# First mixers' attentions: the low part's subtraction issued in the step of the high part's copy

## The reference

```python
def hybrid_mixer(x, w_in, b_in, ...):
    proj = x @ w_in + b_in
    (qa, ka, va, beta_raw, a_raw, za, qb, kb, vb, qc, kc, vc) = jnp.split(proj, split_at, axis=-1)
    o_a = gated_deltanet(qa, ka, va, beta_raw, a_raw, za, conv_w, a_log, dt_bias, gdn_norm_g)
    o_b = chunk_relpos_attention(qb, kb, vb, rel_bias)
    o_c = swa_sink_attention(qc, kc, vc, sinks)
    gates = jax.nn.sigmoid(x @ w_gate + b_gate).reshape(b, t, N_BRANCH, d)
    merged = (gates[:, :, 0] * (o_a @ w_br_a) + gates[:, :, 1] * (o_b @ w_br_b)
              + gates[:, :, 2] * (o_c @ w_br_c))
    return merged @ w_out
```

## Time and profile before

| what | us |
|---|---|
| median of 3 runs | 2250.28 |
| lowest, highest | 2248.72, 2250.85 |
| the profiled execution's own time | 2246.99 |
| span of its instructions | 2245.2 |
| PE busy | 2217.0 (99%) |
| DVE busy | 1632.4 (73%) |
| ACT busy | 1197.9 (53%) |
| attentions of layer 0, first to last subtraction (L1636) | 348.0 to 399.6 |
| attentions of layer 1, the same | some 820 us later |

### The profile page before, as it was taken

One profiled execution on the slowest core, in us unless ns is written; L12 is line 12 of the kernel. 1 busy time (PEld: TensorE's weight loads), 2 busy tenths in 40 slices (PEclk: granted clock), 3 DMA queues, 4 the chain that ended last, 5 costly groups with the idle time before them and its releaser, 6 DMA issues.

```text
span 2245.2 us, 34615 instructions
## 1 busy us (share of the span) xinstructions
PE 2217.0 (99%) x14127; PEld 1903.4 (85%) x14127; DVE 1632.4 (73%) x2508; ACT 1197.9 (53%) x1896; POOL 129.6 (6%) x185
## 2 busy tenths in 40 slices
PE   9999999999999999999999999999999999989999
PEld 7888899878888888888898778888888888867887
DVE  5777768868676776768668867776877678666776
ACT  5555446645555545555356544655554655556653
POOL 2100010120000000000100110000000000420000
PEclk9999999999999999999999999999999999999999
DMA  7755564445556556655554446655655656643654
GB/s 243 226 188 192 188 222 122 146 142 188 190 187 192 187 186 209 192 190 195 196 181 140 140 143 210 196 188 170 215 174 171 213 188 190 200 134 117 197 176 150
DMA packets 284207, 408.17 MB, mean 182 GB/s; under 512 B 13828, under 2 KB 171072, under 8 KB 283792
## 3 DMA queue, kind: packets, MB, share of 16 engines
q1 hardware_dynamic: 276096, 380.84, 52.9%
q0 software_dynamic: 7808, 25.04, 3.8%
q10 hardware_dynamic: 144, 0.07, 0.0%
HBM read 403.98 MB, written 1.91 MB: 181 GB/s over the span
## 4 chain that ended last, share of the span: by engine, by line
PE 91%; DVE 5%; ACT 2%; DMA 1%; issue 1%; POOL 0%; SPq 0%; DVEq 0%; ACTq 0%
PE PS L575 24%; PE PS L506 13%; PE PS L513 12%; PE PS L507 12%; PE PS L574 11%; PE PS L472 3%; PE PS L473 2%; PE PS L474 2%; PE PS L577 2%; PE PS L558 1%; PE PS L556 1%; PE PS L557 1%; PE PS L492 1%; DVE WL L1391 1%; DVE QX L1698 1%; ACT WH L1007 1%
## 5 line engine op out<-in xcount | busy, mean ns | idle before, releaser
L1391 DVE TENSOR_TENSOR WL<-RW,WH 128x1024 fp32r<-128x1024 f32 (+2 forms) x678 | 806.6, 1223 | 160.4 <-ACT WH L1007 156.1
L575 PE MATMUL PS<-XT,WH 128*128 128x512 f32 x2368 | 808.0, 394 | 0.0
L1007 ACT ACTIVATE WH<-RW 128x1024 fp32r<-128x1024 f32 (+2 forms) x678 | 680.5, 1042 | 200.2 <-DMA RW<-in_w_in 40.2
L574 PE MATMUL PS<-XT,WL 128*128 128x256 f32 x2072 | 580.8, 280 | 0.0
L575 PEld LDWEIGHTS PS<-XT,WH 128*128 128x128 f32 x2368 | 425.1, 188 | 76.0
L574 PEld LDWEIGHTS PS<-XT,WL 128*128 128x128 f32 x2072 | 389.8, 188 | 13.4
L506 PE MATMUL PS<-WH,XT 128*128 128x512 f32 (+2 forms) x592 | 229.1, 391 | 1.4 <-DVE WL L1391 0.8
L507 PE MATMUL PS<-WL,XT 128*128 128x512 f32 (+2 forms) x592 | 221.4, 378 | 0.0
L506 PE MATMUL PS<-WH,HTH 128*128 128x512 f32 x488 | 192.7, 395 | 0.0
L507 PE MATMUL PS<-WL,HTH 128*128 128x512 f32 x488 | 191.5, 392 | 0.0
L513 PE MATMUL PS<-WH,XT 128*128 128x512 f32 (+2 forms) x592 | 173.5, 379 | 0.0
(11 more groups left out here) (519 smaller groups left out, 3282.7 us busy)
## 6 DMA issues: line engine op xcount, KB each, us to landing
RW<-in_w_ff_in SPq DMA_DIRECT2D x252, 512.0 KB, 4.4
RW<-in_w_ff_out SPq DMA_DIRECT2D x128, 512.0 KB, 4.4
RW<-in_w_in SPq DMA_DIRECT2D x56, 512.0 KB, 4.6
RW<-in_w_gate SPq DMA_DIRECT2D x48, 512.0 KB, 4.4
RW<-in_ffn_gate SPq DMA_DIRECT2D x44, 512.0 KB, 4.5
RW<-in_ffn_up SPq DMA_DIRECT2D x44, 512.0 KB, 4.6
RW<-in_ffn_down SPq DMA_DIRECT2D x44, 512.0 KB, 4.5
RW<-in_w_out SPq DMA_DIRECT2D x16, 512.0 KB, 4.8
```

The lines of the kernel that those rows point to most:

```text
L574: self.e.matmul(k.PS[:, b.n, 0:T], wl, k.XTH[:, kt, :], start=False, stop=False)
L575: ins = self.e.matmul(k.PS[:, b.n, :], wh, k.XT[:, kt, :], start=kt == 0, stop=kt == 7)
L1007: self.e.activation(u.hi_out, raw, ACT.Copy).then_inc(*self.s["hi"].up(u.n))
L1391: self.e.tensor_tensor(u.lo_out, raw, u.hi_out.bitcast(F), ALU.subtract).then_inc(*self.s["lo"].up(u.n))
```

## The change

In `attention`, `out_lo` with the return of the bank and the entry in `done` is called in the step of `out_hi`. The step behind it is left empty, so that an item has as many steps as before. Nothing else is changed. The mixers of the second block have a generator of their own and are as they were (there the two calls already stand in one step).

```diff
         e.att_out(A, b)
         yield
         e.out_hi(A.id, b, A.nt, A.t0, A.t, hi, lo)
-        yield
         e.out_lo(A.id, b, A.nt, A.t0, A.t, hi, lo)
         self.drop(b, ("turn_lo", A.id))
         done.append(("turn_lo", A.id))
+        yield
         yield
```

## The result

| | before | after |
|---|---|---|
| median of 12 runs each | 2249.39 us | 2254.64 us |
| lowest, highest | 2246.44, 2254.5 | 2250.97, 2258.24 |
| ratio after to before, 95% interval | | 1.0023 [1.0015, 1.0031] |
| the profiled execution's own time | 2246.99 us | 2254.38 us |

The account below looks back on a forecast made before the run. PE was taken as the bound, busy 2217.0 of 2245.2 us, with DVE nearly as full in the attentions. 2 x 1.3 = +2.6 us gave 2249.6 on the profiled execution, 2252.9 on the median; range 2249.0 to 2256.0.

Parts of the forecast that it names:

- Part 1, DVE's order: In each layer's attention, two items' subtractions moved ahead in DVE's queue make DVE late by 0.34 us each, +0.68.
- The high copies' wait: DVE waiting for ACT's high copy before the moved subtraction; bounds nothing and 0.7 us each, taken as nothing.
- Part 2, the banks: Third z-part matmul gets the early-returned bank and waits for its subtraction: +2.14 us, less L621's 0.62, +1.52.
- Part 3, how much stays: Rest of each layer's attention: later waits give back part, leaving PE +1.3 us at the last item's transposes.
- Two small terms, c5's and c6's subtractions: Sixth and seventh items' subtractions stand ahead of later items' L1612/L1614 pairs: +0.23 and +0.2 us.
- The sum: Both layers' attentions: 2 x 1.3 = +2.6 us, 2249.6 on the profiled execution, 2252.9 on the median; chance 50%.
- The mis-sized term: the clock: Rival: TensorE's clock falls at the new wait at 368.6 us, 1.4 us per layer, +2.8, 2255.7; chance 7%.
- The other sign: In another stage, behind two waits close together, the granted clock was 0.50 from 1984 to 1986 us, then 0.79.
- The bank wait in full: Rival: no later wait gives anything back, PE keeps 2.14 us per layer: +4.3, 2254.6; chance 18%.
- The gain: Rival: pool order doesn't bite, PE loses attention waits: -1.2 to -2.6 us, 2247.7 to 2249.1; chance 12%.
- The waits for high copies: Rival: DVE waits 0.7 us each for six items' high copies per layer: +8.4 more, 2261.3; chance 4%.
- nothing: Rival: each loss lies in idle time and the bank is free in time, 2250.3 us; chance 9%.

Follow-up runs that it names:

- f1: Against the kernel before, only the second and third items' subtractions go ahead, every bank returned in the old step; one run, 2251.6 us against 2249.01.
- e2: Against the kernel before, only the bank's return is moved to the high copy's step, the subtraction stays; 2260.48 us, ratio 1.005.
- e3: Against the kernel before, the whole change (subtraction and bank) for the fourth attention item alone; 2249.29 us, ratio 1.0000.
- h2: Against the kernel before, the whole change for the last five of the nine attention items alone; one run, 2252.13 us against 2248.56.
- h1: Against the kernel before, the whole change for the first four of the nine attention items alone; one run, 2252.84 us against 2248.56.
- h0: The changed kernel a third time, no edit; one run, 2251.05 us against 2248.56 of the kernel before.
- second comparison: The changed kernel measured again without an edit, against the kernel before; 2252.82 us against 2250.56, ratio 1.0014.
- f4: Against the kernel before, only the fourth item's subtraction goes ahead, its bank returned late, and z copies issued earlier; 2250.2 us against 2249.01, ratio 1.0002.
- e1: Against the kernel before, subtractions are issued in the high copy's step, banks returned in the old step; 2251.1 us, ratio 1.0005.

## Why the prediction was right, and where it was not

- **Part 1, DVE's order.** Right. L1625 of b1 came at 359.61, which less the 1.09 of the late start is 358.52, as forecast; that of b2 at 366.79 - 1.09 = 365.70, +0.65 for +0.68. f1 showed it alone: +0.68. The high copies' wait, taken as nothing for b1 to c6, is not in DVE's rows for them. It is there for b0, where the prediction said that nothing is lost: 0.64 us, in time in which DVE had been idle for the scores anyway.

DVE's timeline of the changed kernel, answering to the earlier trace rows:

```profile
347.13 0.69 DVE L1636 TENSOR_TENSOR Ob<-PS,Ob 128x512 fp32r<-128x512 f32 x1 [0.64 <-ACT Ob L1092]
348.26 0.69 DVE L1617 TENSOR_REDUCE SX<-PS 128x2 f32<-128x512 f32 x1 [0.44 <-PE PS L634]
...
359.61 0.16 DVE L1625 TENSOR_TENSOR SX<-SX 128x4 f32<-128x4 f32 x1 [0.66 <-ACT PP L1080]
...
366.79 0.16 DVE L1625 TENSOR_TENSOR SX<-SX 128x4 f32<-128x4 f32 x1 [0.38 <-ACT PP L1080]
...
371.20 0.42 DVE L1636 TENSOR_TENSOR Oc<-PS,Oc 128x256 fp32r<-128x256 f32 x1
...
379.62 0.16 DVE L1625 TENSOR_TENSOR SX<-SX 128x2 f32<-128x2 f32 x1 [0.18 <-ACT PP L1080]
...
387.95 0.42 DVE L1584 TENSOR_TENSOR Z<-PS,GB 128x256 f32<-128x256 f32 x1
```

- **Part 2, the banks.** Right: c3's subtraction starts at 371.20 - 1.09 = 370.11 (370.14 forecast), and the third z matmul at 370.58, +2.01 for +2.14; it follows the subtraction's end by 0.05 us and not by 0.15. L621 has no wait and is at +1.44 for +1.52. What was said badly is the size of the wait: "about 2 us" at this one matmul came as 1.20 there and 0.65 more in front of the ALiBi wait. The sum had both in it, because it went by DVE's times and not by the wait. e2 (bank alone) and e3 (c3 alone) tell the two causes apart.
- **Part 3, how much stays.** Right. L1625 of c6 is at +0.79 for +0.88, the z copies at 386.86, +1.00 for +1.1, PE's wait for them is gone, and c8's transposes are at +1.20 for +1.3. The items c4 to c8 alone cost 0.29 per layer (h2). Two small terms, c5's and c6's subtractions of together 0.43, come out at 1.20 - 0.81 = 0.39 between the whole change and h1.
- **The sum.** 2 x 1.2 = +2.4 us of schedule for +2.6. h0, in which the clock did not fall, was +2.5 in time by one run.
- **The mis-sized term: the clock.** The prediction held a fall "unlikely" because PE is dense between the waits "as it was ahead of 1654", with a chance of 7%, and the forecast had nothing for it. It happened in three of ten such stages. Its price was right, 1.5 us for the 1.4 worked out from the earlier trace rows; its frequency and its form were not: it isn't all or nothing, but comes or doesn't by execution. Taken as 3/10 x 2 x 1.5 = 0.9 us in the mean, the loss is 2.4 + 0.9 = 3.3 us, which lies in the second comparison's interval (0.9 to 5.6) and a hair below that of the first (3.4 to 7.0). The step that failed is the reading of the earlier trace rows: that the clock held over the 3 us of standing still was one execution, and in nine traces of thirteen it fell at that place. The other sign was in the prediction too, the fall behind two waits close together (2.16 and 2.25 us). The change made a smaller pair of that form, 0.90 and 1.20 us with two matmuls between them (L506 and L507), by lengthening the first (0.25 before) and adding the second, and my text lumped both into one wait. That the pair is what does it is argued from the count, three stages of ten against none of fourteen. The Trainium skill ("TensorE: Matmul & The Clock Gate", section "HAM oscillation — how this bites in real kernels") has matmuls that stop again and again for their operands fall to the low clock each time; its stops are waits for a DMA of about 3 to 5 us. The traces agree only in part: the pair of 0.90 and 1.20 us lowered the clock in three stages of ten, and the wait of 3.0 to 3.1 us in nine traces of thirteen, not each time.
- **The rivals.** The bank wait in full is refuted as a mechanism: 0.62 and 0.47 are given back. That its time, 2254.6, is the measured median is an accident: the schedule moved by 2.4 us and not by 4.3. The gain is refuted by the wait at the third z matmul; its nearest relative is f4, at most 1.5 us. The waits for high copies and "nothing" are refuted by the rows above.
- **What stays open:** the first comparison's 5.2 us is 1.9 above the 3.3 just worked out. Most of it fits the clock: after's executions had it lower by 0.0012 to 0.0014 in the mean than those of before in the later comparisons, which at 1.7 us for 0.001 is by estimate 2.0 to 2.4 us, and with the schedule's 2.4 gives 4.4 to 4.8. The 12 executions of before in the first comparison have no clock on record, so this isn't shown, nor is how much of it fell in the attentions. Open too is why the clock falls in one execution and not in the next.

## What to carry to other kernels

A reordering that adds and takes no work is a matter of who waits: where two engines are both nearly full, count the delay along the consumer's queue, follow a first-in-first-out pool by hand to see who gets the bank that now comes back earlier, and give back each wait that the delay swallows. Then look at where the remaining waits of TensorE lie to one another: two of about 1 us close together can cost another 1.5 us by the clock, in some executions. And don't take a clock that held in one trace as a sign that it holds: look at the same place in several. Last, judge an edit of 0.1% by a stretch between two fixed instructions in both traces (here exact to 0.02 us), since the time of the whole kernel moved by more than that between two comparisons.

## What the runs showed of the hardware

- The granted clock was 1.00 through a single wait of 1.20 us (e3) and of 1.24 us (e1), and fell to 0.50 behind one of 3.75 us in both layers of e2 and behind 0.90 and 1.20 us in three stages of ten. Behind the pair it was back at 1.00 within 4 us; in layer 1 of e2 it was still 0.50 more than 4 us after PE had started again.
- Behind one wait of 3.0 to 3.1 us (L492, near 1660 us) the clock fell in nine of thirteen traces, and behind waits of about 2.2 and 1.8 to 2.3 us (L943 and L920) in all thirteen. The same wait lowers it in one execution and not in another, so the length of the wait doesn't decide alone.
- Falls of the clock are the larger part of what one execution differs from the next by: the 1030.5 to 1039.9 us behind the attentions are 1028 to 1032 less the work lost to them.
- Each fall behind the pair of waits cost the way 1.5 us (2.71, 2.68 and 2.74 against 1.20, 1.19 and 1.23).
- A subtraction of 256 columns that DVE does earlier moves the rest of its queue by 0.34 us, though it lasts 0.42; and PE's first matmul into the bank followed its end by 0.05 us.
